# A hybrid attention block with expert retrieval: 24 early expert tiles in the retrieval instead of 16, its heads unrolled, and another passage into the expert stage

## The reference

```python
q = (xt @ w_q).reshape(T, PEER_HEADS, 2, PEER_QDIM // 2)            # 8 heads, 2 x 128
s = jnp.einsum('thpd,hpkd->thpk', q, sub_keys)                      # 128 scores per half
s_top, i_top = lax.top_k(s, PEER_TOPK)                              # 16 of 128, twice
# 16 x 16 sums of pairs -> best 16 experts per head, softmax over them
h = jnp.einsum('td,ted->te', xc, jnp.take(u, ic, axis=0))           # hidden of each picked expert
a = jax.nn.gelu(h, approximate=False) * gc
return jnp.einsum('te,ted->td', a, jnp.take(v, ic, axis=0))         # 128 picked rows of v per token
```

## Time and profile before

| | us |
|---|---|
| median of 3 runs (lowest, highest) | 3126.28 (3125.68, 3127.74) |
| the profiled execution, device time | 3127.37 |
| its span, first to last instruction | 3125.7 |
| PE busy in it | 2975.7 (95%) |
| DVE busy | 2313.1 (74%) |
| ACT, POOL busy | 993.3, 1271.3 |
| mean granted PE clock, as a share of full speed | 0.976 |

### The profile page before, as it was taken

The page is one execution under the profiler, slowest core; times in us unless marked ns, Lnnn a source line. Parts: engine busy times, 40 slices in busy tenths (PEclk is TensorE's granted clock), DMA queues, the critical chain, the costliest instruction groups (busy, mean ns, idle before and its releaser), DMA issues.

```text
span 3125.7 us, 48327 instructions
## 1 busy us (share of the span) xinstructions
PE 2975.7 (95%) x17450; PEld 1671.2 (53%) x17450; DVE 2313.1 (74%) x4671; ACT 993.3 (32%) x1420; POOL 1271.3 (41%) x875
## 2 busy tenths in 40 slices
PE   7989998899995999999679999999999999999999
PEld 4445464455553777777445555555555554444444
DVE  3355475369997666666388888888888888999996
ACT  4322364234432555555222222222222222222221
POOL 1013011034333121222266666666655655555562
PEclk9999899999997999999889999999999999999999
DMA  3110101212211455555598888888888878888884
GB/s 99 55 54 14 55 1 34 68 60 75 75 36 68 163 201 190 178 186 195 202 319 275 282 272 273 291 285 274 274 273 284 292 258 285 299 305 297 307 290 170
DMA packets 256176, 594.95 MB, mean 190 GB/s; under 512 B 20768, under 2 KB 127408, under 8 KB 252976
## 3 DMA queue, kind: packets, MB, share of 16 engines
q1 hardware_dynamic: 180016, 318.63, 30.3%
q0 software_dynamic: 73728, 268.47, 24.3%
q10 hardware_dynamic: 2304, 6.29, 0.6%
HBM read 513.63 MB, written 79.69 MB: 190 GB/s over the span
## 4 chain that ended last, share of the span: by engine, by line
PE 43%; DMA 3%; DVE 2%; issue 1%; SPq 1%; ACT 0%; POOL 0%; DVEq 0%; ACTq 0%
PE f_y L238 9%; PE f_y L240 9%; PE f_y L239 9%; PE f_hid L238 5%; PE f_hid L239 5%; PE f_hid L240 5%; DMA f_v_in<-in_peer_v 2%; PE f_u_ps L2181 2%; SPq L2147 1%; DMA f_g_in<-dense_weights 1%; DMA f_rows<-in_peer_u,p_row_index 1%; DVE f_rows L2320 1%; DVE p_h L2330 1%; DVE p_h L2312 0%; DVE f_a_lo L2362 0%
## 5 line engine op out<-in xcount | busy, mean ns | idle before, releaser
L238 PE MATMUL f_y<-f_v_hi,f_a_hi 128*128 128x512 f16 x1536 | 583.1, 380 | 12.8 <-DVE p_h L2312 12.7
L239 PE MATMUL f_y<-f_v_lo,f_a_hi 128*128 128x512 f16 x1536 | 582.9, 379 | 0.0
L240 PE MATMUL f_y<-f_v_hi,f_a_lo 128*128 128x512 f16 x1536 | 582.7, 379 | 0.0
L2279 POOL DMA_INDIRECT f_rows<-in_peer_u,p_row_index x256 | 354.2, 1383 | 210.2 <-DVE f_rows L2320 128.5
L2279 POOL DMA_INDIRECT f_rows<-in_peer_v,p_row_index x256 | 310.6, 1213 | 286.0 <-DVE p_h L2330 256.8
L2320 DVE SCALAR_TENSOR_TENSOR f_rows<-f_rows,p_xs 128x1024 f32<-128x1024 f32 x256 | 380.2, 1519 | 50.2 <-DMA f_rows<-in_peer_u,p_row_index 50.2
L2330 DVE SCALAR_TENSOR_TENSOR p_h<-f_rows,f_row_a,p_h 128x1024 f32<-128x1024 f32 x256 | 397.9, 1554 | 20.8 <-DMA f_rows<-in_peer_v,p_row_index 13.9
L2312 DVE SCALAR_TENSOR_TENSOR p_h<-f_y,p_h 128x512 f32<-128x512 f32 x384 | 263.2, 685 | 105.6 <-PE f_y L240 103.3
L2290 POOL TENSOR_TENSOR f_v_lo<-f_v_in,f_v_hi 128x1024 f16<-128x1024 f32 x128 | 281.3, 2197 | 143.9 <-ACT f_v_hi L2254 142.6
L238 PE MATMUL f_hid<-p_act_hi,x_u_hi 128*128 128x384 f16 x1008 | 330.4, 328 | 2.0 <-DVEq L2297 2.0
L239 PE MATMUL f_hid<-p_act_lo,x_u_hi 128*128 128x384 f16 x1008 | 330.4, 328 | 0.0
(11 more groups left out here) (314 smaller groups left out, 5343.0 us busy)
## 6 DMA issues: line engine op xcount, KB each, us to landing
f_v_in<-in_peer_v SPq DMA_DIRECT2D x128, 512.0 KB
dense_weights<-e_stage SPq DMA_DIRECT2D x24, 2048.0 KB, 8.6
f_g_in<-dense_weights SPq DMA_DIRECT2D x32, 1536.0 KB
x_u_in<-in_peer_u SPq DMA_DIRECT2D x64, 512.0 KB
e_u_in<-in_peer_u SPq DMA_DIRECT2D x48, 512.0 KB
x_gel<-early_tiles SPq DMA_DIRECT2D x64, 384.0 KB
early_tiles<-e_gel SPq DMA_DIRECT2D x48, 384.0 KB, 2.5
a_w_in<-in_w_in SPq DMA_DIRECT2D x24, 512.0 KB, 3.7
```

The source lines that it names most:

```text
L238: pe.matmul(out, a_hi, b_hi, start=first, stop=False)
L239: pe.matmul(out, a_hi, b_lo, start=False, stop=False)
L240: return pe.matmul(out, a_lo, b_hi, start=False, stop=last)
L2279: nc.gpsimd.indirect_dma_start(out=rows[q % ROWS][:], out_offset=None, in_=table, in_offset=bass.IndirectOffsetOnAxis(ap=T.row_index[:, ti ...
```

## The change

- `retrieve`: `EARLY_R * PEER_H` = 16 tiles become `N_RETRIEVE` = 24, by heads 2, 3, 2, 3, 3, 2, 3 and 6. All heads are written out instead of looped. On POOL the match products of head h - 1 come in step h, after the first low part and the low part of the query weights; the weights of head h - 1 come after the low part of the step's second tile. On DVE the sum of weights (`totals`) of head h - 1 comes after the first top 16 of head h. On ACT the exponential (`weigh`) comes after the step's second tile, in the last head after the fifth.
- `spread_weights`: the buffers of early tiles are a ring of 2 instead of 4. DVE and POOL are written out. The rows of `peer_u` for the first five row jobs are fetched at its end into buffers allocated earlier, and the rows of expert tiles 2 and 3 past the early ones are loaded there too.
- `experts`: 56 late tiles and 72 early ones. The weights of the first group are loaded first. No row jobs stand in the first four steps; 368 are spread over the 52 other late steps, 144 over the early ones. ACT's and DVE's first steps have another order.

```diff
+HEAD_TILES = (2, 3, 2, 3, 3, 2, 3, 6)
+N_RETRIEVE = sum(HEAD_TILES)
+N_EARLY = N_RETRIEVE + EARLY_S * NBLOCK
...
         @block.tensor
...
+            for h in range(PEER_H):
+                of_head = tiles(h)
+                E.turn(pe, *of_head[0])
+                if h + 1 < PEER_H:
+                    queries(h + 1, (h + 1) % 2)
+                    scores(h + 1)
+                for i, (c, b) in enumerate(of_head):
+                    E.hidden(pe, c, b, 0)
+                    if i + 1 < len(of_head):
+                        E.turn(pe, *of_head[i + 1])
+                    E.hidden(pe, c, b, 1)
+            pe.wait_ge(index_done, 2 * PEER_H)
...
         @block.scalar
...
+                for i, (c, b) in enumerate(of_head):
+                    E.gelu(act, c, b, 0)
+                    if i + 1 < len(of_head):
+                        E.split(act, *of_head[i + 1])
+                    E.gelu(act, c, b, 1)
+                    E.keep(act, c, b)
+                    if i == (len(of_head) - 2 if h + 1 == PEER_H else 1):
+                        weigh(h)
...
         @block.gpsimd
...
+            for h in range(PEER_H):
+                of_head = tiles(h)
+                E.low(pool, *of_head[0])
+                if h + 2 < PEER_H:
+                    low_w(h + 2, h % 2)
+                if h:
+                    picks(h - 1)
+                for i, (c, b) in enumerate(of_head[1:]):
+                    E.low(pool, c, b)
+                    if h and i == 0:
+                        weights(h - 1)
+            picks(PEER_H - 1)
+            weights(PEER_H - 1)
...
-        E = EarlyTiles(nc, io, T, S, EARLY_S, EARLY_R * PEER_H, EARLY_S * NBLOCK)
+        E = EarlyTiles(nc, io, T, S, EARLY_RING, N_RETRIEVE, EARLY_S * NBLOCK)
...
                 for b in range(EARLY_S):
-                    E.keep(sp, blk, b)
-                    if not last:
-                        E.load(sp, blk + 1, b)
+                    if b + EARLY_RING + 1 < EARLY_S or not last:
+                        E.load(sp, *ring_at(blk, b + EARLY_RING + 1))
+                    E.keep(sp, *ring_at(blk, b))
...
+            for b in range(2):
+                rows = slice((N_EARLY + 2 + b) * P, (N_EARLY + 3 + b) * P)
+                sp.wait_ge(next_turned, b + 1)
+                sp.dma_start(F.u_in[b][:], io.peer_u[0, rows, :]).then_inc(next_loaded, 16)
...
-            return min(JOBS, 6 * late + 2 * early)
+            return min(JOBS, SPREAD_JOBS + LATE_JOBS * max(late - GROUP, 0) // (EARLY_FROM - GROUP) + 2 * early)
...
                 for m in range(LOOP):
                     n = c * LOOP + m
-                    if m % GROUP == 0 and not (first and m == 0):
+                    if m % GROUP == 0:
                         load_g(m // GROUP, n)
...
+                    elif first and 2 <= m < LOOP - 2:
+                        load_u(n + 2, m + 2)
...
+            hi_u(2, 2)
+            hi_v(0)
+            gelu(1)
+            hi_u(3, 3)
+            hi_v(1)
+            hi_v(2)
+            hi_a(0)
+            hi_a(1)
...
+            lo_u(2, 2)
+            lo_u(3, 3)
             for n in range(NE):
                 step(n)
```

More of the change, by code:

```diff
@@ L1339 @@
 EARLY_S = 4
+EARLY_RING = 2
+ROWS = 5
+SPREAD_JOBS = 0
 BLOCK = 64
@@ L1511, in retrieve, with tiles @@
         block = ctx.enter_context(nc.Block())
-        PAIRS = PEER_H // 2
+        def tiles(h):
+            n = sum(HEAD_TILES[:h])
+            return [divmod(i, EARLY_R) for i in range(n, n + HEAD_TILES[h])]
         @block.sync
@@ L1519, in load_w @@
                 sp.dma_start(w_in[:], w_v[h]).then_inc(w_loaded, 16)
-            def step(hh, b, first=False, last=False):
-                h = 2 * hh + b
-                if not last:
-                    sp.wait_ge(w_lo_done, h + 2)
-                    load_w(h + 2)
-                if not (first and b == 0):
-                    E.load(sp, h, 1)
-                if not (last and b):
-                    E.load(sp, h + 1, 0)
             sp.sem_inc(w_loaded, 16)
@@ L1535, in _ @@
             load_w(1)
-            for b in range(2):
-                step(0, b, first=True)
-            with sp.Fori(1, PAIRS - 1) as hh:
-                for b in range(2):
-                    step(hh, b)
-            for b in range(2):
-                step(PAIRS - 1, b, last=True)
-            E.all_kept(sp, EARLY_R * PEER_H)
+            for h in range(PEER_H):
+                if h + 2 < PEER_H:
+                    sp.wait_ge(w_lo_done, h + 2)
+                    load_w(h + 2)
+                for c, b in tiles(h):
+                    if c + 1 < N_RETRIEVE // EARLY_R:
+                        E.load(sp, c + 1, b)
+            E.all_kept(sp, N_RETRIEVE)
         @block.tensor
@@ L1710, in low_w, with picks @@
                 nc.gpsimd.tensor_tensor(w_lo[slot][:], w_in[:], w_hi[slot][:], ALU.subtract).then_inc(w_lo_done, 1)
[L1712 to L1723 removed]
+            def picks(h):
                 for n in range(2):
@@ L1900, in spread_weights @@
         F = T.first
+        row_loaded = [S.sem(f"row_loaded{b}") for b in range(ROWS)]
+        row_used = S.sem("row_used")
         next_loaded = S.sem("next_loaded")
@@ L2022, in _, with fetch @@
             E.prime_gpsimd(pool)
-            with pool.Fori(0, NBLOCK) as blk:
-                for b in range(EARLY_S):
-                    E.low(pool, blk, b)
+            def fetch(q):
+                if q >= ROWS:
+                    pool.wait_ge(row_used, q - ROWS + 1)
+                nc.gpsimd.indirect_dma_start(
+                    out=F.rows[q % ROWS][:], out_offset=None, in_=io.peer_u[0],
+                    in_offset=bass.IndirectOffsetOnAxis(ap=T.row_index[:, 0, q:q + 1], axis=0)).then_inc(
+                        row_loaded[q % ROWS], 16)
+            BLOCKS_TILES = EARLY_S * NBLOCK
+            fetched = 0
+            for n in range(BLOCKS_TILES):
+                E.low(pool, *ring_at(n // EARLY_S, n % EARLY_S))
+                upto = SPREAD_JOBS * (n + 1) // BLOCKS_TILES + ROWS if SPREAD_JOBS or n + 1 == BLOCKS_TILES else 0
+                for q in range(fetched, upto):
+                    fetch(q)
+                fetched = max(fetched, upto)
+            for b in range(ROWS):
+                pool.wait_ge(row_loaded[b], 16 * (SPREAD_JOBS // ROWS + 1))
         @block.sync
@@ L2058 @@
 NE = NKEYS
-ROWS = 5
 def experts(nc, io, T):
@@ L2077, in experts @@
         v_lo = [[S.sb(f"v_lo{g}{j}", [P, D], F16) for j in range(GROUP)] for g in range(2)]
-        rows = [S.sb(f"rows{b}", [P, D]) for b in range(ROWS)]
-        row_hid = S.sb("row_hid", [P, NS, PICKS])
+        rows, row_hid = T.first.rows, T.row_hid
         row_a = S.sb("row_a", [P, NS, PICKS])
@@ L2282, in fetch @@
                         row_loaded[q % ROWS], 16)
-            for q in range(ROWS):
-                fetch(q)
             for n in range(NE):
@@ L2434, in allocate_first @@
     F.gel = [S.sb(f"gel{b}", [P, DSEQ], side="right") for b in range(2)]
+    F.rows = [S.sb(f"rows{b}", [P, D], side="right") for b in range(ROWS)]
     return F
```

267 lines of the change are left out of this document (105 added, 162 removed).

## The result

The changed kernel takes 3082.19 us (median of 4 runs, 3081.31 to 3085.94), the kernel before, run beside it, 3127.01 (3125.68 to 3134.03). The ratio is 0.9854, with a 95% interval of 0.9837 to 0.9872: 1.5% faster. The prediction said 3079, in 3062 to 3112. The profiled execution took 3081.31 us with a span of 3079.6, against 3127.37 and 3125.7 before.

What follows compares the result with a forecast made beforehand. PE was taken as the bound nearly throughout, with DVE also full in retrieval and DMA fullest in the passage. The span 3125.7 - 68.3 + 60 - 42 + 3 = 3078.4 gave a 3079 us median, range 3062 to 3112.

Steps and rivals of the forecast that it cites:

- Late and early steps: Expert stage: eight late steps of 16.44 us become early ones of 7.9 us, net -68.3 us (-70 to -67).
- The extra jobs: Late steps: 7.08 row jobs a step instead of 6, +3 us in all (0 to +26).
- Retrieval: Retrieval stage: eight more tiles, +46.3 us before the last step and +13.5 in it, +60 (+52 to +70).
- DVE's lag: Retrieval: DVE runs 48 us behind a step's start, but the lag doesn't grow; no cost taken.
- Spreading: Spreading stage: a ring of 2 tile buffers and added loads at the end, 0 us (-2 to +3).
- Passage: First expert steps up to step 5: no row jobs, tiles already there, weights first; -42 us (-34 to -46).
- The eight tiles alone are worth 8 us: Moving eight tiles from late to early, across retrieval and expert stage: a gain of 8 us, the rest from the passage.
- A: Rival, late steps: DVE becomes the pace at 16.9 us a step, 3099 us; chance 0.12.
- B: Rival, late steps: the row ring sets the pace once a buffer's round passes 11.6 us, up to 3141 us; chance 0.06.
- C: Rival, retrieval: every step waits 6 us for DVE's lag, +42, 3121 us, no change; chance 0.05.
- D: Rival, last head and stage starts: stalls behind POOL vanish and the clock stays up, -20, 3059 us; chance 0.06.
- E: Rival, late steps: DVE blocks every row fetch on POOL, 18.2 us a step, +91, 3167 us; chance 0.03.

Runs made afterwards that it cites:

- experiment 8: Changed kernel with two early tiles for every head (16) and POOL's weights of the head before right behind its picks: 3098.11 us.
- experiment 3: Changed kernel with the 368 late row jobs spread over all 56 late steps from the first on, instead of over 52: 3123.75 us.
- experiment 9: Changed kernel with the earlier kernel's 16 early tiles (1, six times 2, 3) and POOL's weights right behind the picks: 3085.13 us.
- the ring of four: Changed kernel with four row buffers instead of five: 3168.02 us.
- experiment 6: Changed kernel with the third and fourth tile loaded at the start of the expert stage, not at the end of the spreading: 3097.51 us.
- experiment 11: Changed kernel with weights right behind picks, last head's products and exponential a tile earlier, 75 row jobs in spreading, one per early step: 3082.03 us.

## Why the prediction held, step by step

- **Late and early steps (-68.3).** 51 steps of 16.51 us and 76 parts of 7.95: -128.2 + 62.6 = -65.6 with the extra jobs' cost in it, against -65.3. The extra jobs, taken at +3, are (16.51 - 16.44) x 51, some 3.5 us in this profile; kernels with the same late code differ by up to 8 us, so that the 3.5 fits so well is in part luck. DVE is busy 15.0 us a step as worked out; a fetch on POOL takes 1.29 us, less than the 1.41 assumed. Row waits come where they were expected, in the steps of a group's weights (24.5 and 11.4 us in all), and PE takes under 3 us of them.
- **Retrieval (+60), measured +62.6.** First step 44.1, inner two-tile steps 42.2, three-tile steps 51.5 to 52.3: these made +50.2 of a predicted +46.3 (336.9 against 286.7 from the first turn to the last step's). The first step has 1.8 us of the difference (PE waits 2.27 us for its second low part), three of the four three-tile steps 0.8 each (the table load of experiment 8); the prediction priced every tile alike at 9.24. The last step took 64.2 us where 65.3 was forecast (13.5 more than before; it was 12.4). One argument in it was wrong, and its number right by luck: the second low part wasn't held behind head 6's products. POOL waited 0.85 us for ACT in front of it; its hidden matmuls started 16 us into the step, as forecast, because PE turned the second tile only at 10.7 us. The products are 7.64 us, not the 8.53 of the earlier trace rows. A single one takes 3.83 us; the first of the older pair took 4.74, begun while DVE was still at the second match, the other 3.83. Why is not shown.
- **DVE's lag (costed at nothing).** With 24 tiles it is: head 7's matches are found at 1027.4, 38 us into the last step (as forecast), and POOL asks at 1042.5. With two tiles for every head it costs 6.6 us. It was the right rival to fear, with the wrong number of tiles.
- **Spreading (0), measured -1.2.** Within the kernels' scatter.
- **Passage (-42), measured -43.6**, with PE waiting 1.5 us before step 4 where 2 was forecast. The sum and the chain (weights, gel multiplications, low part, turn) were right. What the prediction didn't weigh is the shares: it gave rows and weights as one sum, and the runs give the rows 34 to 40 us by themselves and the weights' place none, once tiles and rows come from the stage before. The prediction spoke of rows that block DVE; experiment 3 shows mostly the jobs' own DVE time (37.9 us more) and less the waits for rows (12.3). My first expectation after the result put the jobs at 11 to 26 us, less than 26 jobs take on DVE by themselves.
- **"The eight tiles alone are worth 8 us; the passage makes the gain."** 5.5 us by the stages of experiment 9, not told apart from none by the times; the passage alone takes the time to 3085.
- **Rivals.** A (DVE sets late steps) would show turns 16.9 us apart; they are at 16.51. B is bounded by the ring of four: the round is 10.3 us by that estimate, decision at 11.6. C shows at 16 tiles only, with 6.6 us in the last step. D's recovered clock is there in part: the last head's window has 0.97 for 0.80 and the passage 1.00 for 0.79, and it was already in the forecast of both, since both assumed PE with hardly a wait. E is refuted by the 1.29 us of a fetch.

The Trainium skill, "SBUF — State Buffer", section "SBUF: two separate sides", says that GpSimd and a DVE operation with two SBUF inputs exclude each other for a whole instruction. The trace after agrees in single cases, as DVE's and POOL's timelines show: a row job of 3.22 us and not 1.22, beside POOL's low part.

```profile
1901.30 3.22 DVE L2332 SCALAR_TENSOR_TENSOR x_rows<-x_rows,p_xs 128x1024 f32<-128x1024 f32 x1
```

```profile
1901.29 2.13 POOL L2301 TENSOR_TENSOR f_v_lo<-f_v_in,f_v_hi 128x1024 f16<-128x1024 f32 x1
```

The prediction took the transfers that GpSimd issues into the rule. The Trainium skill says that, in the same section, of DVE operations in a two-port mode. Here, of 361 row fetches in the late steps, the 73 with no DVE operation on two SBUF inputs beside them take 0.93 to 0.94 us on POOL and the others up to 1.97. Neither sets the pace, since with seven jobs for six the late step grew by 0.07 us.

## What to carry to other kernels

An engine that works in order makes all that stands behind a job wait, both for the job's own time and for what is left of its row's latency. Here 26 jobs at the start of a stage cost 37.9 us of the first and 12.3 of the second, and the passage took nearly all of it, while seven jobs a step later on cost next to nothing beside a full PE. At the start of a stage, put such work behind the first results, and price it by its count times its own time before you look at latency. Moving equal work between two stages that one engine fills brings what the price per piece differs by, here 16.5 against 9.25 + 7.95, which is no gain; only pieces laid into a step that waits anyway are free. Undo one part at a time and then leave one part alone: 3.5 and 9.2 us for the same loads say that they matter only once the larger cause is gone.

## What the runs showed of the chip that I had not expected

- After a wait of 5.53 us PE ran at half pace, matmuls 0.32 us apart instead of 0.16, for 5.7 us (experiment 6). The same wait of 4.38 us, in the last head's step, was followed by some 2.7 us of half pace in the changed kernel and 5.9 in experiment 11. After the wait of 1.47 us in the changed kernel's passage the granted clock stays at 1.00.
- A table load on ACT ahead of a gelu, 1.28 us, lengthened the step by 0.85 us, because the high part of the next tile stands behind it (experiments 8 and 11).
- A round of a row buffer, fetch to reuse, is 10.3 us (estimated from the ring of four) at 283 GB/s of all transfers; the DVE waits for rows total 138.5 us with four buffers and 35.9 with five, at seven rows a step.
- Cutting DVE's work in the early steps from 545 to 374 us gave 6.6 us of 604, though DVE was busy 90% of them.
- Stages with the same code differ between kernels: the late steps took 840.9 to 848.7 us in seven of them. A difference of 5 us between two versions can't be read from one profile.
